# A hybrid decoder trunk on eight cores: later places for work behind loads, a norm block in R's rows, and X asked for ahead of stores

## The reference

```python
def _layer(x, ...):
    h = _rmsnorm(x, norm1_g)
    z = h @ w_in            # columns [zb | zc | zv | zu | ga | gs]
    conv_out, new_buf = _conv_causal(zc * zv, conv_buf, conv_w, conv_b)   # depthwise, width 3
    ya = zb * conv_out
    ys, hr, hi = _s5(zu, h0_re, h0_im, ...)   # 32 groups of 16 channels, each a complex diagonal state of 64
    gy = gelu(ys); ys = gy * sigmoid(gy @ w_glu + b_glu)
    m = sigmoid(ga) * (ya @ w_branch[:512]) + sigmoid(gs) * (ys @ w_branch[512:])
    x = x + m @ w_out
    h2 = _rmsnorm(x, norm2_g)
    gate, up = split(h2 @ w_gate_up)          # 2816 each
    return x + (silu(gate) * up) @ w_down, new_buf, hr, hi
```

## Time and profile before

| what | value |
|---|---|
| median of three runs (lowest, highest) | 3977.66 us (3686.79, 4197.6) |
| profiled execution | 3685.78 us |
| its span (slowest core, core 5) | 3684.0 us |
| spans of all cores | 3677.5 to 3684.0 us, mean clock 0.982 to 0.987 |
| PE busy | 3531.0 us, 96% of the span |
| DVE, ACT, POOL busy | 1969.2, 1194.1, 274.5 us |
| chain that ended last | PE 90%, DMA 3%, issue 2%, DVE 2% |

### The profile page before, as it was taken

The page is one execution under the profiler, slowest core; times in us unless marked ns, Lnnn a source line. Parts: engine busy times, 40 slices in busy tenths (PEclk is TensorE's granted clock), DMA queues, the critical chain, the costliest instruction groups (busy, mean ns, idle before and its releaser), DMA issues.

```text
span 3684.0 us, 65802 instructions; the slowest of 8 cores (3677.5 to 3684.0 us)
## 1 busy us (share of the span) xinstructions
PE 3531.0 (96%) x23936; PEld 1970.0 (53%) x23936; DVE 1969.2 (53%) x3510; ACT 1194.1 (32%) x2263; POOL 274.5 (7%) x531
## 2 busy tenths in 40 slices
PE   4799999999999999999979999999999999999998
PEld 1444444444444444444446666666666666666665
DVE  5847337472555627365355572655627456374323
ACT  4424223341334323242233332334323342233212
POOL 1000000000000000000000000000000000000000
PEclk9899999999999999999989999999999999999999
DMA  5244444344444434354454343344434444333343
GB/s 115 49 75 70 78 71 78 69 75 70 75 78 81 75 64 72 71 99 76 74 130 78 69 83 65 64 88 73 75 64 70 82 74 77 58 73 70 68 79 80
DMA packets 99530, 279.51 MB, mean 76 GB/s; under 512 B 14352, under 2 KB 25488, under 8 KB 99216
## 3 DMA queue, kind: packets, MB, share of 16 engines
q0 software_dynamic: 72576, 243.30, 38.7%
q1 hardware_dynamic: 26640, 32.00, 2.8%
HBM read 508.55 MB, written 9.98 MB: 141 GB/s over the span
## 4 chain that ended last, share of the span: by engine, by line
PE 90%; DMA 3%; issue 2%; DVE 2%; ACT 2%; SPq 1%; DVEq 0%; ACTq 0%
PE ps L401 90%; DMA PRS<-chd 1%; ACT SCR L405 1%; DVE R L412 1%; DMA X<-xp 1%; DMA GS<-cst 0%; SPq L390 0%; ACT L405 0%; ACT R L405 0%; DMA R<-xp 0%; SPq L384 0%; DVE PRS L412 0%; DMA CIN<-xp 0%; DVE SCR L418 0%; DVE H L418 0%
## 5 line engine op out<-in xcount | busy, mean ns | idle before, releaser
L401 PE MATMUL ps<-H,RING 128*128 128x512 bf16 (+2 forms) x12160 | 2184.0, 339 | 49.9 <-ACT SCR L405 17.6
L401 PEld LDWEIGHTS ps<-H,RING 128*128 128x128 bf16 x12160 | 1181.1, 98 | 991.0 <-issue 83.3
L401 PE MATMUL ps<-R,RING 128*128 128x512 bf16 (+2 forms) x6400 | 1184.2, 338 | 4.9 <-ACT SCR L405 3.2
L405 ACT ACTIVATE SCR<-ps 128x384 f32<-128x384 f32 (+2 forms) x824 | 419.8, 514 | 1580.4 <-PE ps L401 1508.0
L401 PEld LDWEIGHTS ps<-R,RING 128*128 128x128 bf16 x6400 | 621.5, 98 | 495.4 <-issue 15.5
L412 DVE TENSOR_TENSOR R<-SCR,ps 128x272 bf16<-128x272 f32 (+2 forms) x520 | 296.2, 582 | 602.9 <-PE ps L401 563.6
L452 POOL DMA_DIRECT2D RING<-wseq x504 | 266.2, 528 | 3365.7 <-PE ps L401 3241.1
L412 DVE TENSOR_TENSOR X<-X,ps 128x512 f32<-128x512 f32 (+2 forms) x480 | 280.2, 584 | 406.3 <-PE ps L401 403.5
L412 DVE TENSOR_TENSOR SCR<-SCR,ps 128x512 f32<-128x512 f32 (+2 forms) x304 | 173.9, 581 | 261.2 <-PE ps L401 228.6
L405 ACT ACTIVATE H<-X 128x512 bf16<-128x512 f32 (+2 forms) x352 | 189.0, 543 | 287.1 <-DVE X L412 273.6
L412 DVE TENSOR_TENSOR PRS<-PRS 128x256 f32<-128x256 f32 (+2 forms) x391 | 194.0, 505 | 81.5 <-DMA PRS<-chd 56.9
(11 more groups left out here) (90 smaller groups left out, 1266.6 us busy)
## 6 DMA issues: line engine op xcount, KB each, us to landing
RING<-wseq POOLq DMA_DIRECT2D x376, 512.0 KB, 6.1
RING<-wseq POOLq DMA_DIRECT2D x64, 384.0 KB, 4.8
RING<-wseq POOLq DMA_DIRECT2D x64, 320.0 KB, 4.1
X<-xp SPq DMA_DIRECT2D x8, 512.0 KB
PRS<-chd SPq DMA_DIRECT2D x32, 128.0 KB
yp<-SCR SPq DMA_DIRECT2D x16, 256.0 KB, 10.3
yp<-SCR SPq DMA_DIRECT2D x16, 192.0 KB, 2.0
GS<-bst SPq DMA_DIRECT2D x8, 256.0 KB
```

The lines of the kernel that those rows point to most:

```text
L401: return S.op("pe", lambda e: e.matmul(out, lhsT=lhsT, rhs=rhs, start=start, stop=stop, **kw), reads=reads, writes=writes, mode=pmode(lhsT ...
L405: return S.op("act", lambda e: e.activation(out=out, in_=in_, func=func, **kw), reads=reads, writes=writes, cost=180.0 + 0.83 * numel(out) ...
```

## The change

Six things. `finalize` assumes more time for a load: the landing is 3500 ns instead of 1900, and loads above 100,000 bytes (400,000 before) go through the pipe, at 260 bytes per ns. Three operations get a key more to wait for: the negation of half of GS (cst) is placed behind AB, and SSTB, the first product of SST and SCVW behind FFN0, which the first product of an FFN writes. The final norm's second block in half 0 writes its eight results into R's rows as f32 instead of SCR slots. In half 0 the final norm's stores come after all eight loads of X of their block, and they read a key FGY which the block's last STT writes. The samples' x is loaded at the start into X's columns 1024 to 1040, and ACT copies it to columns 640 to 656 at the change of halves. The last loads of X there (columns 656 to 1040) wait for the last norm row of the third block.

```diff
--- before.py
+++ after.py
@@ -176,10 +176,10 @@
                 end += 100.0
             free[e] = end
             if o.sem is not None:
-                if o.nbytes > 400000:
-                    pipe = max(pipe, end) + o.nbytes / 230.0
+                if o.nbytes > 100000:
+                    pipe = max(pipe, end) + o.nbytes / 260.0
                     end = pipe
-                end += 1900.0
+                end += 3500.0
             for x in succ[i]:
                 lat = 60.0 if x.eng == e else 90.0
                 if end + lat > ready[x.pos]:
@@ -663,7 +663,7 @@
             act(BXB[h, :, :, 16 * g2:16 * g2 + 16], v4(w[cu])[h], AF.Copy, kW[cu], ["BXB"])
             yield
 
-        ts(stc[:, 1, :], stc[:, 1, :], -1.0, None, ALU.mult, ALU.bypass, kC + ["FFN0"], kC)
+        ts(stc[:, 1, :], stc[:, 1, :], -1.0, None, ALU.mult, ALU.bypass, kC + ["FFN0", "AB"], kC)
         yield
         src, ks = stc, kC
         for m in range(9):
@@ -698,7 +698,7 @@
     def sample_loads(l):
         load(SST[:], sst_in[l], ["SST"])
         load(SCV[:], scv_in[l], ["SCV"])
-        act(SSTB[:], SST[:], AF.Copy, ["SST"], ["SSTB"])
+        act(SSTB[:], SST[:], AF.Copy, ["SST", "FFN0"], ["SSTB"])
         store(sconv_o[l, :, 0], SCV[:, 1], ["SCV"])
 
         ar = bc(AB[:, 0, 16 * l:16 * l + 16], [[1, 16], [0, NS]])
@@ -708,11 +708,11 @@
         t2 = SCR[:, i, 256:512].rearrange("p (q t) -> p q t", t=NS)
         kk = sk(i)
         for ri in range(2):
-            tt(t1, SST[:, ri], ar, ALU.mult, ["SST", "AB"], kk)
+            tt(t1, SST[:, ri], ar, ALU.mult, ["SST", "AB", "FFN0"], kk)
             tt(t2, SST[:, 1 - ri], ai, ALU.mult, ["SST", "AB"], kk)
             tt(SNEW[:, ri], t1, t2, ALU.subtract if ri == 0 else ALU.add, kk, ["SNEW"])
         w = [bc(pcol("cw", l * 12 + 4 * z), [[1, 4], [0, NS]]) for z in range(2)]
-        tt(SCVW[:], SCV[:, 1], w[1], ALU.mult, ["SCV", "PT"], ["SCVW"])
+        tt(SCVW[:], SCV[:, 1], w[1], ALU.mult, ["SCV", "PT", "FFN0"], ["SCVW"])
         t3 = SCR[:, i, 0:64].rearrange("p (q t) -> p q t", t=NS)
         tt(t3, SCV[:, 0], w[0], ALU.mult, ["SCV", "PT"], kk)
         tt(SCVW[:], SCVW[:], t3, ALU.add, kk + ["SCVW"], ["SCVW"])
@@ -756,6 +756,7 @@
 
     def norm_block(gname, gidx0, out_h, c0, n, half=None, held=None):
         st["nb"] = 13 - st["nb"]
+        outs = []
         fgk = ["FG"] if st["xh"] and c0 and gidx0 == 0 and out_h else []
         xk = [xv_(kt, c0, n) for kt in range(8)] if held is None else held
         act(EPSC[:, 2:3], EPSC[:, 0:1], AF.Ln, ["EPSC"] + xk[0][1] + fgk, ["EPSD"])
@@ -775,21 +776,29 @@
                 continue
             if kt == 0:
                 st["scr"] = (i + 1) % NSCR
-            o = scr()
-            if o == i:
+            if half == 0 and c0:
+                ov, ok = R[:, kt, :].bitcast(F32), gk("R", kt, 0, NCOL)
+            else:
                 o = scr()
-            stt(SCR[:, o, 0:n], xv, pcol(gname, gidx0 + kt), SCR[:, i, 0:n], ALU.mult, ALU.mult,
-                xk[kt][1] + ["PT"] + sk(i), sk(o))
+                if o == i:
+                    o = scr()
+                ov, ok = SCR[:, o, :], sk(o)
+            stt(ov[:, 0:n], xv, pcol(gname, gidx0 + kt), SCR[:, i, 0:n], ALU.mult, ALU.mult,
+                xk[kt][1] + ["PT"] + sk(i), ok + (["FGY"] if kt == 7 else []))
             n0 = min(n, 1024 - c0)
-            if n0 > 0:
-                store(yp[half, :, kt, c0:c0 + n0], SCR[:, o, 0:n0], sk(o))
-            if n0 < n:
-                store(ysm[:, kt, :], SCR[:, o, max(n0, 0):n], sk(o))
             if half == 0:
+                outs.append((kt, ov, ok))
                 if c0 == 0:
                     load(X[:, kt, 0:512], xp[1, :, kt, 384:896], xseg(kt, 0, 512))
                 else:
                     load(X[:, kt, 512:640], xp[1, :, kt, 896:1024], xseg(kt, 512, 128))
+                continue
+            if n0 > 0:
+                store(yp[half, :, kt, c0:c0 + n0], ov[:, 0:n0], ok)
+            if n0 < n:
+                store(ysm[:, kt, :], ov[:, max(n0, 0):n], ok)
+        for kt, ov, ok in outs:
+            store(yp[0, :, kt, c0:c0 + n], ov[:, 0:n], ok + ["FGY"])
 
     YA, YS, UT = 0, 4, 8
     MT = [4, 5, 6, 7, 12, 13, 14, 15]
@@ -1173,6 +1182,7 @@
         if bi == 0:
             issue_unit(xl[1:2])
             issue_unit(xl[2:3])
+    load(X[:, :, 1024:1040], xs[:, :, :], [("X", kt, 5) for kt in range(8)])
     for i in range(2, NSLOT):
         issue_unit(xl[4 + min(i - 2, 3):5 + min(i - 2, 3)])
     params()
@@ -1195,12 +1205,12 @@
 
         ffn(half, l, tail)
         if half == 0 and l + 1 == DEPTH:
-            load(X[:, :, 640:656], xs[:, :, :], [("X", kt, 3) for kt in range(8)])
+            act(X[:, :, 640:656], X[:, :, 1024:1040], AF.Copy, [("X", kt, 5) for kt in range(8)], [("X", kt, 3) for kt in range(8)])
             st["xh"] = 1
             for (c0, n) in blocks(1)[1:]:
                 norm_block("n1", 0, True, c0, n)
             for kt in range(8):
-                load(X[:, kt, 656:1040], xp[1, :, kt, 0:384], xseg(kt, 656, 384))
+                load(X[:, kt, 656:1040], xp[1, :, kt, 0:384], xseg(kt, 656, 384), reads=gk("H", 7, *blocks(1)[2]))
     store(hc_o[:, :, :, :], HC[:], [("HC", l_, f) for l_ in range(DEPTH) for f in range(4)])
     store(pconv_o[:, :, :, :], CONVST[:], [("CONVST", l_, f) for l_ in range(DEPTH) for f in range(4)])
     fin = list(S.last_dma.values())
```

## The result

The changed kernel takes 3648.48 us (median of four runs, 3644.03 to 3650.03); its profiled execution took 3647.31, with a span of 3645.8 on core 2. To the kernel before, both in undisturbed runs (some runs of before are far longer, so its plain median says nothing), the ratio is 0.989, interval 0.9867 to 0.9914; on another chip later 0.9877, 0.9855 to 0.9898. The forecast was 3645, and 3645 to 3685.8 is 0.989. So the time came out as forecast. What follows asks whether it did so for the reasons given.

What follows compares the result with a forecast made beforehand. PE, busy 3531.0 of 3684.0 us, was taken to bound the kernel, leaving 153 us of waits. Gains 18 + 9.3 + 2.1 + 2.3 + 9 = 40.7 took 3685.8 to 3645 us, range 3627 to 3668.

Steps and rivals of the forecast that it cites:

- Assumed load costs and the rest: Remaining order changes throughout the kernel: move operations inside stretches where PE does not wait; gain nothing.
- the term for half 1: Half 1, ahead of the GLU's result: SCVW moved into the FFN removes conv-state waits; gain 2.3 us, bounds 0 and 3.6.
- Startup: Start to first GLU: DVE's cst and chd waits go, PE resumes near 95; gain 18 us, bounds 6.3 and 23.1.
- The table load of gelu: Startup: a table load now falling directly ahead of the GLU, costing about 3 us.
- xs at the start: Startup queue: early xs moves the seventh X load between 1.1 us earlier and 4.3 later; taken as no difference.
- The rivals on xs: Startup: xs packets behind weight packets delay X loads; total 3651, or 3663 if the whole startup gain goes; chance 0.10.
- Layer 3 and its FFN: Half 0: SSTB's wait ahead of the GLU goes, gain 9.3 us; the FFN's chd read-back wait goes, gain 2.1.
- The change of halves: Between halves: X loads ahead of stores let PE resume near 1864.7 instead of 1874.06; gain 9 us, bounds 0 and 25.9.
- The chain that I gave for the new order: Change of halves: X loads land 6.8 us earlier, stores by 1859.7, then the eighth final-norm product, last load, PE near 1864.7.
- Preparation that sinks too low: Rival, mixers: longer assumed loads make convolution kernels late, seven preparations overrunning by 10 us; total 3715, chance 0.02.
- the seventh load: Startup: the seventh X load, needed for the fourteenth square, lands between 1.1 us earlier and 4.3 later.
- mean-packet bound: Startup: xs as 64 packets per engine at 0.09 us each costs at most 5.8 us of the queue.

Runs made afterwards that it cites:

- e1: Kernel before with only the three longer assumed load costs in finalize; ratio 0.9912 to the kernel before.
- e2: Changed kernel with the old assumed load costs, keys, norm block and xs kept as changed; ratio 0.9921 to the kernel before.
- e5: Changed kernel with xs loaded at the change of halves again, behind the stores of R; ratio 0.9894 to the kernel before.
- e6: Changed kernel with the old norm block and xs loaded at the change of halves again; ratio 0.9893 to the kernel before.
- e7: Changed kernel with all X loads of the change of halves ahead of all stores of y; ratio 0.9857 to the kernel before, median 3640.98 us.
- e8: Changed kernel run again without any edit; ratio 0.9877 to the kernel before.
- e3: Changed kernel without the key FFN0 on SSTB, the first product of SST and SCVW; ratio 0.9877 to the kernel before.
- e4: Changed kernel with the old norm block (second block in SCR slots, stores and loads in turn); ratio 0.9896 to the kernel before.
- e9: Kernel before with one edit: the last eight X loads, of 384 columns, wait for the third block's last norm row; ratio 0.9992 to before.
- e11: Changed kernel with all stores behind all X loads, plus the copy of the transposes on ACT instead of DVE; ratio 0.9861 to the kernel before.

## Why the prediction was right, and where it was not

The orders were priced rightly at the start, in layer 3 and at the change of halves. Two steps failed. "Assumed load costs and the rest", said to "move operations inside stretches in which PE does not wait", were put at "Nothing": alone on the kernel before they give the whole gain at the start and most of that in layer 3, 32 us of the 41 (e1, ratio 0.9912). And the term for half 1, 2.3 us, did not come: none was measured.

**Startup, 18 forecast, 20.1 measured** (186.4 to 166.3). Right in size and way: both DVE waits gone, one long PE wait, ended at 92.60 where I had 95. The transposes came at 33.4 to 37.2 on the cores, for which I had 36.1. Misread was which edit does it. I wrote of the negation as moved by the change and priced the new order as a whole, which was right for the order; but e1 shows that the assumed costs alone give all of it (186.4 to 164.3), and the key gives nothing more. With the key and old costs (e2) 7.6 of the 20 are left. The table load of gelu, put at about 3 us without a row, leaves PE idle for 1.89 ahead of the GLU.

**xs at the start, nothing forecast, 0.3 to 3.6 us lost by the pair compared** (e5 and e6 against e7 and e8 on one chip, e1 against e3 and e4 on another), inside the bounds of 1.1 gained and 4.3 lost. The rivals on xs, 3651 and 3663, did not happen. The Trainium skill ("DMA: Bandwidth & Descriptors", Queues, rings and completion order) has each DMA engine serve its queues in turn, a packet of each; a weight packet's wait for every packet of xs, 64 x 0.365 = 23 us, is not what these runs show. By the same section of the Trainium skill a packet typically holds some 9 to 17 descriptors, so the rule does not ask for 23 us unless each 64-byte record of the trace is a whole packet; no run here shows which it is.

**Layer 3 and its FFN, 11.4 forecast, 12.0 measured** (1649.7 to 1637.7). Right; the costs are enough for it without FFN0 (e3), and FFN0 is enough for the wait ahead of the GLU without the costs (e2).

**The change of halves, 9 forecast, 9.5 measured; the shares of the edits were misread.** The chain that I gave for the new order is what the trace shows: squares 6.8 us earlier counted from the last 512-column sum (15.2 after it instead of 22.0), stores landed 22.2 after it (forecast 23.2), then the eighth product, then PE. The norm block in R's rows, to which I gave the gain, is worth 2.2 next to the other edits (e4) and costs 3.5 with xs late (e5 against e6). What made the stretch long before is how late SP asks for xs. Taking xs out of this place is worth 7.4 to 8 us in the changed kernel (e5 against the two runs of the changed kernel) and 1.7 with the old norm block (e6 against e4). With xs left there, the loads of the last 384 columns count, since half of them stood ahead of it: 5 us alone (e9) and 8 with the new costs (e1 against e6). I costed these loads at nothing in the new order, which no run contradicts, and gave no price to their old place. So the sum was right since I had priced the new order from its end; the share of each edit was not.

**Half 1, 2.3 forecast, none measured** (1581.3 to 1581.9): this term failed. I read it from the slowest core alone. Its three gaps (1.39, 0.74 and 1.51 us, the second in the earlier trace rows) have their like on cores 0, 4 and 6 of the kernel before; on cores 1, 2, 3 and 7 there are none. After, only one gap of 1.05 is left, on cores 2 and 5 each: PE's waits of 0.3 us and more in half 1 add up to 19.0 to 22.9 us by core before, median 20.9, and to 18.8 on five of eight cores after, which is also the median. The time also holds things that the term left out. On core 0, which has no group at the lower clock in either profile, half 1 falls by 2.2 us with two gaps of 1.25 and 1.12. On core 6 a gap of 0.73 goes, but two of the 56-matmul groups of e8 begin at the lower clock where none did before, 10.19 us instead of 8.51 each, and half 1 grows by 2.3. And on cores 2 and 4 PE stood up to 2.79 and 2.24 us with nothing in the profile to wait for, as in the first row here; the second is a group at the lower clock.

```profile
2355.97 0.98 PE L401 MATMUL ps<-H,RING 128*128 128x272 bf16 x7 [2.79 <-issue]
...
2363.57 10.19 PE L401 MATMUL ps<-H,RING 128*128 128x272 bf16 x56 [1.72 <-ACT R L405]
```

Such a wait at this place stands on three of the sixteen cores of the changed kernel's two profiles. On these three the last 16 KB packet of queue q8, of kind "instruction", ahead of the wait's end came 16.3 to 16.8 us behind the one before it; on the other thirteen the same packet came 6.4 to 10.7 us behind. That PE waited for instructions fits this, but no run tests it.

**The sum:** 20.1 + 12.0 + 9.5 - 0.6 = 41.0 against 40.7; the median core's span fell by 40.4 (3680.7 to 3640.3). That it is so near is luck in part: the terms are off by +2.1, +0.6, +0.5 and -2.9, and these cancel. Three slips in the working change little: the chain at the change of halves adds up to 1864.4 and not 1864.7, the seventh load with xs at nothing would land 1.5 us earlier and not 1.1, and the gaps of half 1 are 0.7 to 1.5 and not 1.0 to 1.5. Of the rivals none happened. Preparation that sinks too low would have shown as waits for KF or WBF in the mixers, and there are none.

## What to carry to other kernels

Where a scheduler fixes the order from assumed times, look for what it assumes of loads first: here three constants (which of them does it was not separated) moved the operations that stood ahead of their loads, and the hand-made keys then gave nothing more. Price a new order from its last wait, but learn the share of an edit only by taking it out, since edits on one queue are not independent. On a shared queue find the load that is waited for last, here 64 KB of samples, and ask what can wait behind it: the largest further gain among these runs was to put all stores behind all loads that are needed first.

## What was not expected

An operation that was freed from one wait came too early for the next: in e11 DVE gave back 6.9 us in two new waits of 3.6 and 3.8. And 64 KB in 1024 small packets cost the start 0.3 to 3.6 us, under what their mean-packet bound allowed (5.8), but more than the nothing that I took.
